# Putting the gate block of the first group ahead of its row tiles, in the opening of a hybrid decoder kernel

## The chip, the cores and the metric

The kernel runs on one core of a Trainium2 chip. The metric is the device time of one execution in microseconds. All weights and activations are float32 in memory. The engines named below are TensorE (PE, its weight loads PEld), VectorE (DVE), ScalarE (ACT), GpSimd (POOL) and SyncE (SP), which issues the weight loads.

## What is computed

The reference is a two-layer decoder trunk on 256 tokens of width 2048: a Mamba-2 layer, an MLP, an attention layer with a sliding window, an MLP, each followed by a layer norm. Only the start matters here, the Mamba-2 mixer:

```python
zxbcdt = h @ w_in                     # (256 x 2048) @ (2048 x 10304)
z   = zxbcdt[..., :D_INNER]           # the gate
xbc = zxbcdt[..., D_INNER:D_INNER + CONV_DIM]
dt_raw = zxbcdt[..., D_INNER + CONV_DIM:]
xbc = jax.nn.silu(conv(xbc) + conv_b) # causal, 4 taps, per channel
dt  = jax.nn.softplus(dt_raw + dt_bias)
...                                   # scan in two chunks of 128 tokens
y = y * jax.nn.silu(z)
```

The channels fall into 8 groups. Each has 128 channels of B, 128 of C, 512 of xs and 512 of z. The 64 values of dt are needed by all groups.

## The kernel before

**Products in split float32.** Each operand is split into a high part, which is the value rounded to the type fp32r, and a low part, the rest. A product is high times high, high times low and low times high. The weights pass in chunks of 128 x 1024 values (512 KB): SP loads chunk k into one of four slots of `raw` (L346 to L354), ACT copies it to `whi` (L818), DVE subtracts to get `wlo` (L1249), PE uses it. `whi` and `wlo` are rings of eight chunks. The semaphore `w_split` counts chunks that DVE has finished. SP waits for it before it loads into a slot again, so the load of chunk k is issued once chunk k - 4 is split; PE waits for it in `chunk()` (L426). ACT splits chunk k (`step`, L820) once PE has used chunk k - 8 (`w_used`).

**Two kinds of product.** `row_tile` (L431) makes 128 output channels for all 256 tokens in one PSUM bank, from two chunks: 16 matmuls of 512 columns (L451) and 16 of 256 columns (L457). Its weight chunk holds 8 blocks of 128 rows x 128 columns, so its load moves in pieces of 512 B. `column_block` (L481) makes 512 channels, tokens on partitions, in two banks, from eight chunks of 256 rows x 512 columns; `column_chunk_products` (L461) issues twelve matmuls of 512 columns for each (L476 to L478). Row tiles give B, C, xs and dt, column blocks give z.

**The opening.** PE first multiplies zeros (L552), then turns x: the input lies in SBUF as tokens x channels, and PE transposes it in tiles of 128 x 128 (L528) into PSUM, from where ACT writes its high part and DVE its low part to `actA` (`x_hi` L838, `x_lo` L1272). `x_transposes(g)` (L532) turns one quarter of x, 512 channels of both token halves, eight transposes into two banks. Quarters 0 and 1 are turned before the first product, 2 and 3 inside the first row tile. SP issues x quarter 0, the identity, chunk 0, quarters 1 and 2, chunk 1, quarter 3 (L366 to L379), then waits for quarter 2 before chunk 2. POOL waits for quarter 2 before it issues its nine small loads of vectors (L1970 on).

**The first group** (PE L620, ACT L940, DVE L1457): row tiles for B, C and dt, four for xs, then the z block. The first row tiles add their low products chunk by chunk (`lo_last=False`). Inside the second tile PE transposes the small vectors (L538). Between the chunks of the z block it transposes dt (`dt_transposes`, after chunk 0), makes its sums over time (`dt_sums`, after chunk 4), and transposes those (`cs_transposes`, after chunk 6).

What follows a row tile is a chain: ACT copies the half of the bank with the cross products (`cross`, L888), DVE adds the other half, which frees the bank (`conv_sum`, L1368), DVE runs the four taps (`conv`, L1375), ACT takes the tanh, DVE makes the silu (`silu`, L1392). xs tiles alternate between banks 0 and 1. For dt: `dt_cross` and `dt_add` (L1315), PE transposes, `softplus` on DVE (L1322 to L1354, some 18 small operations one after the other), PE's `dt_sums`, DVE's copy (L1356), PE's `cs_transposes`, then POOL writes the sums to memory and reads them back spread over all partitions (L1950). For z: ACT takes the tanh (`z_tanh`, L905), DVE multiplies (`z_out`, L1397).

Each engine's order is written out by hand, as a list of `step()` (one chunk's split) and these pieces. An engine that waits in one piece holds up all that is listed behind it.

**The later groups** (`group`, PE L631, ACT L985, DVE L1503): six row tiles, then the z block. After its first row tile a group takes the `s1` products of the group before (L586), which need all six `silu` of that group. After its fourth it takes the scan products (L595), which need ACT's `decay` (L915), which needs the sums read back by POOL. The z of the group before is taken through tanh at the head of the next group.

Of the kernel before, what the change touches and what calls it, by code (L numbers as in the profile page):

```python
# [29 lines left out]
P = 128  # L30
T = 256
# [95 lines left out]
def build(nc, t, out):  # L127
# [57 lines left out]
    per_head_in = nc.alloc_semaphore("per_head_in")  # L185
    x_in = [nc.alloc_semaphore(f"x_in{g}") for g in range(4)]
# [7 lines left out]
    by_dma = {keys_doubled, rows_out, rows_in, *loaded, *x_in, ident_in, consts_in, vectors_in, per_head_in, x_again_in, gains_in, out_done}  # L194
# [118 lines left out]
    def group_chunks(g, first=False):  # L313
        cols = [COL_B + g * DS, COL_C + g * DS] + [COL_XS + g * GW + i * P for i in range(4)]
        if first:
            cols.insert(2, COL_DT - NHD)
        for c in cols:
            for r in range(2):
                yield t["w_in"], r * CH, c, P
        for r in range(8):  # L320
            yield t["w_in"], r * 2 * P, COL_Z + g * GW, BLK
# [16 lines left out]
    with block:  # L338
# [3 lines left out]
        def _(e):  # L342
# [18 lines left out]
            def load_x(g):  # L361
                cols = slice(g * BLK, (g + 1) * BLK)
                e.dma_start(xin[:, :, cols], t["x"][0, :, cols].rearrange("(h p) n -> p h n", p=P)).then_inc(
                    x_in[g], C.up(x_in[g]))

            def load_first_group():  # L366

                load_x(0)
                e.dma_start(ident[:, :], t["consts"][:, K_ID:K_ID + P]).then_inc(ident_in, C.up(ident_in))
                for k, args in enumerate(group_chunks(0, first=True)):  # L370
                    load(*args)
                    if k == 0:
                        load_x(1)
                        load_x(2)
                    if k == 1:
                        load_x(3)
                        e.wait_ge(x_in[2], C.now(x_in[2]))
# [37 lines left out]
        def _(e):  # L415
# [15 lines left out]
            def row_tile(b, act, ready={}, inside={}, first=False, lo_last=True):  # L431
# [5 lines left out]
                for h in range(2):  # L437
                    if first and h == 0:
                        s = 0
                        e.wait_ge(first_split, C.next(first_split))  # L440
                    else:
                        s = chunk()
                    for k in range(8):
                        kt = 8 * h + k
                        if first and kt == 4:
                            s = chunk()
# [14 lines left out]
            def column_chunk_products(b0, act, c, ready=0, inside={}, second_half=None):  # L461
# [3 lines left out]
                s = chunk()  # L465
                order = [(k, h) for h in range(NH) for k in range(2)] if second_half else [
                    (k, h) for k in range(2) for h in range(NH)]
                for i, (k, h) in enumerate(order):
                    if i in inside:
                        inside[i]()  # L470
                    if i == 2 and second_half:
                        second_half()
                    kt = 2 * c + k
# [58 lines left out]
            def x_transposes(g):  # L532
                e.wait_ge(x_in[g], C.next(x_in[g]))
                for h in range(NH):
                    transposes(2 + (2 * g + h) % 6,
                               [xin[:, h, (4 * g + i) * P:(4 * g + i + 1) * P] for i in range(4)], counted=False)
# [21 lines left out]
            zero_products(8)  # L558
# [249 lines left out]
        def _(e):  # L808
# [29 lines left out]
            def x_hi(g):  # L838
                for h in range(NH):
                    b = 2 + (2 * g + h) % 6  # L840
# [1227 lines left out]
```

## Time and profile before

| | before |
|---|---|
| median of 3 runs | 2385.74 us (2385.48 to 2387.28) |
| the profiled execution | 2385.26 us |
| its span in the trace | 2383.1 us |
| PE busy | 2366.2 us, 99% |
| VectorE busy | 1576.4 us, 66% |
| ScalarE busy | 1168.7 us, 49% |
| weight loads | 818 of 512 KB |
| DMA traffic | 455 MB, mean 191 GB/s |

The profiled execution has 2.2 us outside its span. PE's busy share is near the whole, so time can only be won or lost where PE stands still or where it does something other than the products. All times in the rows are counted from the start of the span.

### The profile page before, as it was taken

What the parts mean: (1) busy time and instruction counts of PE and PEld (TensorE: products, weight loads), DVE (VectorE), ACT (ScalarE), POOL (GpSimd) and SP (SyncE); (2) the same over time, 40 slices, a digit from 0 to 9 for tenths busy, and PEclk for the clock granted to TensorE, in tenths of its full rate; (3) what the DMA queues carried; (4) which work ended last, traced back from release to release, by engine and by line L of the source; (5) the groups of instructions that cost most, each with busy time, mean ns of one, the idle gap of its engine ahead of it and who ended that gap; (6) DMA issues with size and microseconds to landing.
All of it is one profiled execution on the core that took longest, in us unless ns stands there. A gap on an engine that the chain in (4) does not pass through costs nothing.

```text
span 2383.1 us, 32530 instructions
## 1 busy us (share of the span) xinstructions
PE 2366.2 (99%) x12610; PEld 1999.4 (84%) x12610; DVE 1576.4 (66%) x2151; ACT 1168.7 (49%) x1742; POOL 40.8 (2%) x85
## 2 busy tenths in 40 slices
PE   9999999999999999999999999999999999999998
PEld 8888888888888888888888888778888888888886
DVE  7888888885568556556556577766864654655655
ACT  5555555564355444445344355774543443443441
POOL 0000000000000000000000000000000000000000
PEclk9999999999999999999999999999999999999999
DMA  8766666657667666666666646446776666666663
GB/s 235 228 195 194 187 192 189 190 171 238 194 187 234 210 189 189 197 187 188 198 189 188 200 153 203 125 124 202 199 232 188 190 196 184 192 198 188 191 195 109
DMA packets 487826, 455.08 MB, mean 191 GB/s; under 512 B 13792, under 2 KB 360080, under 8 KB 485392
## 3 DMA queue, kind: packets, MB, share of 16 engines
q1 hardware_dynamic: 484608, 433.51, 61.2%
q0 software_dynamic: 3088, 19.79, 2.4%
q8 instruction: 88, 1.44, 0.3%
q14 instruction: 42, 0.34, 0.0%
HBM read 450.55 MB, written 2.16 MB: 190 GB/s over the span
## 4 chain that ended last, share of the span: by engine, by line
PE 92%; DVE 3%; ACT 2%; DMA 1%; issue 1%; SPq 0%; POOL 0%; DVEq 0%; ACTq 0%
PE ps L451 25%; PE ps L476 15%; PE ps L477 15%; PE ps L478 15%; PE ps L457 13%; PE ps L509 2%; PE ps L507 2%; PE ps L508 2%; DVE wlo L1249 1%; PE ps L528 1%; ACT whi L818 1%; PE ps L600 1%; ACT pb L1172 0%; DMA csb<-cs_rows 0%; ACT em L920 0%
## 5 line engine op out<-in xcount | busy, mean ns | idle before, releaser
L1249 DVE TENSOR_TENSOR wlo<-raw,whi 128x1024 fp32r<-128x1024 f32 x817 | 994.4, 1222 | 670.2 <-ACT whi L818 669.0
L818 ACT ACTIVATE whi<-raw 128x1024 fp32r<-128x1024 f32 x817 | 859.6, 1057 | 852.5 <-PE ps L478 447.9
L451 PE MATMUL ps<-actA,whi 128*128 128x512 f32 x2704 | 648.2, 391 | 0.8 <-DVE wlo L1249 0.5
L451 PEld LDWEIGHTS ps<-actA,whi 128*128 128x128 f32 x2704 | 497.1, 188 | 98.6 <-issue 0.9
L476 PE MATMUL ps<-whi,actB 128*128 128x512 f32 x1056 | 412.7, 391 | 0.0
L477 PE MATMUL ps<-wlo,actB 128*128 128x512 f32 x1056 | 411.0, 389 | 0.0
L478 PE MATMUL ps<-whi,actB 128*128 128x512 f32 x1056 | 410.9, 389 | 0.0
L457 PEld LDWEIGHTS ps<-actA,wlo 128*128 128x128 f32 x2704 | 347.2, 191 | 13.5
L457 PE MATMUL ps<-actA,wlo 128*128 128x256 f32 x2704 | 351.3, 283 | 0.0
L476 PEld LDWEIGHTS ps<-whi,actB 128*128 128x128 f32 x1056 | 198.3, 188 | 42.7 <-issue 1.3
L478 PEld LDWEIGHTS ps<-whi,actB 128*128 128x128 f32 x1056 | 198.3, 188 | 41.3
L477 PEld LDWEIGHTS ps<-wlo,actB 128*128 128x128 f32 x1056 | 198.3, 188 | 40.3
L476 PE MATMUL ps<-whi,actA 128*128 128x512 f32 x544 | 215.9, 397 | 1.0 <-DVE actA L1261 1.0
L478 PE MATMUL ps<-whi,actA 128*128 128x512 f32 x544 | 212.0, 390 | 0.0
L477 PE MATMUL ps<-wlo,actA 128*128 128x512 f32 x544 | 212.0, 390 | 0.0
L476 PEld LDWEIGHTS ps<-whi,actA 128*128 128x128 f32 x544 | 102.1, 188 | 23.6 <-issue 2.5
L478 PEld LDWEIGHTS ps<-whi,actA 128*128 128x128 f32 x544 | 102.1, 188 | 21.8
L477 PEld LDWEIGHTS ps<-wlo,actA 128*128 128x128 f32 x544 | 102.3, 188 | 19.6
L832 ACT ACTIVATE actB<-fsq 128x256 fp32r<-128x256 f32 x120 | 50.2, 418 | 109.9 <-DVE fsq L1727 109.9
L1578 DVE TENSOR_TENSOR res<-ps,res 128x512 f32<-128x512 f32 x80 | 51.9, 686 | 63.0 <-PE ps L509 32.6
L903 ACT ACTIVATE thb<-xh 128x256 f32<-128x256 f32 x48 | 19.9, 415 | 123.8 <-DVE xh L1389 123.8
L1727 DVE SCALAR_TENSOR_TENSOR fsq<-fb 128x256 f32<-128x256 f32 x120 | 51.0, 425 | 4.1
(209 smaller groups left out, 1679.5 us busy)
## 6 DMA issues: line engine op xcount, KB each, us to landing
raw<-in_mlp_w SPq DMA_DIRECT2D x512, 512.0 KB, 4.5
raw<-in_a_w_in SPq DMA_DIRECT2D x162, 512.0 KB, 4.6
raw<-in_a_w_out SPq DMA_DIRECT2D x64, 512.0 KB, 4.7
raw<-in_b_w_q SPq DMA_DIRECT2D x32, 512.0 KB, 5.1
raw<-in_b_w_o SPq DMA_DIRECT2D x32, 512.0 KB, 4.1
csb<-cs_rows POOLq DMA_DIRECT2D x8, 1024.0 KB, 6.9
raw<-in_kv_w SPq DMA_DIRECT2D x16, 512.0 KB, 4.0
gb<-in_ln_g POOLq DMA_DIRECT2D x4, 1024.0 KB, 7.8
```

Of the source, the lines that this page charges most:

```text
L451: e.matmul(ps[:, b, :], whi[:, s, k * P:(k + 1) * P], act[:, kt, :, :].rearrange("p a n -> p (a n)"), start=(kt == 0), stop=False)
L457: last = e.matmul(ps[:, b, T:2 * T], wlo[:, slots[half], k * P:(k + 1) * P], act[:, kt, 0, :], start=False, stop=(kt == KT - 1))
L476: e.matmul(ps[:, b0 + h, :], act[:, kt, 0, tk], whi[:, s, w], start=(kt == 0), stop=False)
L477: e.matmul(ps[:, b0 + h, :], act[:, kt, 0, tk], wlo[:, s, w], start=False, stop=False)
L478: last = e.matmul(ps[:, b0 + h, :], act[:, kt, 1, tk], whi[:, s, w], start=False, stop=(kt == KT - 1))
L507: e.matmul(ps[:, b0 + h, :], act[:, kt, 0, tk], hi_w, start=(kt == 0), stop=False)
L508: e.matmul(ps[:, b0 + h, :], act[:, kt, 0, tk], lo_w, start=False, stop=False)
L818: e.activation(whi[:, s, :], raw[:, r, :], ACT.Copy).then_inc(w_hi_done, C.up(w_hi_done))
L832: e.activation(dst, src, ACT.Copy).then_inc(act_hi_done, C.up(act_hi_done))
L1249: e.tensor_tensor(wlo[:, s, :], raw[:, r, :], whi[:, s, :].bitcast(F32), ALU.subtract).then_inc(w_split, C.up(w_split))
L1578: ins = e.tensor_tensor(r, ps[:, b, :], r, ALU.add)
L1727: e.scalar_tensor_tensor(fsq[:, i % 2, :], fb[:, i % 2, :], 0.0, fb[:, i % 2, :], ALU.max, ALU.mult).then_inc(f_squared, C.up(f_squared))
```

## The change

In the first group the z block comes first, then the row tiles in the order dt, B, C, xs 0 to 3. x is turned in eight pieces of 256 channels (four transposes into one bank), the first two before the first product and each later one in front of the chunk before its use. The first x piece and the first half of chunk 0 are loaded separately. dt's transposes follow B, its sums follow xs 0, their transposes follow xs 1. All row tiles now add their low products last. In the second group the z pieces fall away, since z of the first is taken inside the first group.

```diff
 def group_chunks(g, first=False):
     cols = [COL_B + g * DS, COL_C + g * DS] + [COL_XS + g * GW + i * P for i in range(4)]
...
+    z = [(t["w_in"], r * 2 * P, COL_Z + g * GW, BLK) for r in range(8)]
+    rows = [(t["w_in"], r * CH, c, P) for c in ([COL_DT - NHD] if first else []) + cols for r in range(2)]
+    yield from z + rows if first else rows + z
...
 SP, load_first_group
-    load_x(0)
-    e.dma_start(ident[:, :], ...)
-    for k, args in enumerate(group_chunks(0, first=True)):
-        load(*args)
-        if k == 0:
-            load_x(1)
-            load_x(2)
-        if k == 1:
-            load_x(3)
-            e.wait_ge(x_in[2], C.now(x_in[2]))
+    chunks = list(group_chunks(0, first=True))
+    load_x(slice(0, 2 * P), x_first_in)
+    load_first_half(0, first_loaded)
+    e.dma_start(ident[:, :], ...)
+    load_first_half(1, loaded[0])
+    load_x(slice(2 * P, 4 * P), x_in[0])
+    for k in range(1, 4):
+        load(*chunks[k])
+        load_x_quarter(k)
+    for k in range(4, len(chunks)):
+        load(*chunks[k])
...
 PE
+def x_transposes(m):
+    ...
+    transposes(4 + m % 4, [xin[:, h, (2 * m + i) * P:(2 * m + i + 1) * P] for i in range(2) for h in range(NH)],
+               counted=False)
 x_transposes(0)
-zero_products(8)
+zero_products(4)
 x_transposes(1)
+def first_z_block():
+    fill(2)
+    fill(3)
+    for c in range(8):
+        if 0 < c < 7:
+            x_transposes(c + 1)
+        column_chunk_products(2, actA, c, 1, first=(c == 0))
 def first_group():
-    row_tile(0, actA, ready={0: 2, 4: 2, 8: 2, 12: 2}, first=True, lo_last=False,
-             inside={2: lambda: x_transposes(2), 7: lambda: x_transposes(3)})
-    row_tile(1, actA, inside={8: vector_transposes}, lo_last=False)
-    row_tile(4, actA, lo_last=False)
-    for i in range(4):
-        row_tile(i % 2, actA, lo_last=i > 0)
-    column_block(2, actA, after={0: [dt_transposes], 4: [dt_sums], 6: [cs_transposes]})
+    first_z_block()
+    row_tile(4, actA, inside={8: vector_transposes})
+    row_tile(0, actA)
+    dt_transposes()
+    row_tile(1, actA)
+    row_tile(0, actA)
+    dt_sums()
+    row_tile(1, actA)
+    cs_transposes()
+    row_tile(0, actA)
+    row_tile(1, actA)
...
 ACT and DVE, opening
+for m in range(1, 6):
+    x_hi(m)            # DVE: x_lo(m)
+    split_weights()
+for m in (6, 7):
+    x_hi(m)            # DVE: x_lo(m)
+    step()
...
 ACT, first_group, as it stands after the change
+for _ in range(6):
+    step()
+z_tanh(8)
+step(); step()
+dt_cross(10); step(); constants_out(); step()
+cross(0, 12); step(); tanh(0); dt_exp(); step()
+cross(1, 14); step(); tanh(1); step()
+cross(2, 16); step(); tanh(2); dt_decays(); step()
+cross(3, 18); step(); tanh(3); dt_cs2(); step()
+cross(4, 20); step(); tanh(4); step()
+cross(5, 22); tanh(5)
...
 DVE, first_group, as it stands after the change
+for _ in range(6):
+    step()
+z_out()
+step(); step()
+vectors_out()
+...                    # cwg copy
+dt_add()
+step(); step()
+conv(0, 0); step()
+softplus(); step()
+silu(0, 0); conv(1, 0); step(); step()
+silu(1, 0); conv(2, 0); dt_sums(); step(); step()
+silu(2, 0); conv(3, 0); rotations_out(); step(); step()
+silu(3, 0); conv(4, 0); step(); step()
+silu(4, 0); conv(5, 0); silu(5, 0)
```

(The two lists of ACT and DVE are written several calls to a line here; in the file each stands on its own line.)

## Rows read from the trace of the kernel before

**Rows 1.** The page: span, and busy time with share of the span.
```profile
span 2383.1 us, 32530 instructions
PE 2366.2 (99%) x12610; PEld 1999.4 (84%) x12610; DVE 1576.4 (66%) x2151; ACT 1168.7 (49%) x1742; POOL 40.8 (2%) x85
```

**Rows 2.** Timeline, 1 to 10 us: start, duration, engine, line, operation, count, idle before.
```profile
1.07 4.52 PE L552 MATMUL ps<-st 128*128 128x128 f32 x24 [1.07 <-DVE st L1279]
...
5.43 1.04 PE L528 MATMUL ps<-ident,xin 128*128 128x128 f32 x8
6.07 1.09 ACT L832 ACTIVATE actA<-ps 128x512 fp32r<-128x512 f32 x2 [4.03 <-PE ps L528]
...
6.77 1.29 DVE L1261 TENSOR_TENSOR actA<-ps,actA 128x512 fp32r<-128x512 f32 x2 [5.74 <-ACT actA L832]
7.04 0.63 ACT L846 ACTIVATE whi<-raw 128x512 fp32r<-128x512 f32 x1
...
7.98 1.28 DVE L1284 TENSOR_TENSOR wlo<-raw,whi 128x512 fp32r<-128x512 f32 x2
...
8.49 1.09 PE L528 MATMUL ps<-ident,xin 128*128 128x128 f32 x8 [0.24 <-DMA xin<-in_x]
...
9.34 0.71 PE L451 MATMUL ps<-actA,whi 128*128 128x512 f32 x2
```

**Rows 3.** Timeline of PE: the vectors' transposes, a row tile, block and groups beginning.
```profile
20.94 0.48 PE L542 MATMUL ps<-ident,vst 48*128 48x48 f32 x5
...
21.79 2.12 PE L451 MATMUL ps<-actA,whi 128*128 128x512 f32 x8
...
42.34 3.82 PE L451 MATMUL ps<-actA,whi 128*128 128x512 f32 x16
...
53.48 0.40 PE L476 MATMUL ps<-whi,actA 128*128 128x512 f32 x1
...
76.50 3.79 PE L451 MATMUL ps<-actA,whi 128*128 128x512 f32 x16
...
137.96 3.79 PE L451 MATMUL ps<-actA,whi 128*128 128x512 f32 x16
...
198.64 1.52 PE L451 MATMUL ps<-actA,whi 128*128 128x512 f32 x6
```

**Rows 4.** Timeline of ACT, second group: the wait for the sums read back.
```profile
91.80 2.45 ACT L920 ACTIVATE em<-csb,csg 128x128 f32<-128x128 f32 x8 [1.00 <-DMA csb<-cs_rows]
```

**Rows 5.** Windows, 6 to 8 us: length, busy of each engine, PEclk, DMA share, GB/s.
```profile
6.00:8.00 2.00, 2.00 (x21) 2.00 (x19) 1.23 (x3) 1.93 (x4) 0.00 (x0) 1.00 1.02 356
```

**Rows 6.** Timeline of SP and ACT, 67 to 80 us: a load and three waits of ACT.
```profile
67.72 0.37 SPq L351 DMA_DIRECT2D raw<-in_a_w_in  x1
...
71.78 1.06 ACT L818 ACTIVATE whi<-raw 128x1024 fp32r<-128x1024 f32 x1 [2.22 <-DMA raw<-in_a_w_in]
74.41 1.06 ACT L818 ACTIVATE whi<-raw 128x1024 fp32r<-128x1024 f32 x1 [1.56 <-DMA raw<-in_a_w_in]
...
79.41 1.06 ACT L818 ACTIVATE whi<-raw 128x1024 fp32r<-128x1024 f32 x1 [0.53 <-DMA raw<-in_a_w_in]
```

**Rows 7.** Timeline of DVE: pieces of its list.
```profile
22.14 0.21 DVE L1299 TENSOR_SCALAR cw<-ps 128x32 f32<-128x32 f32 x1
...
24.18 0.42 DVE L1382 TENSOR_SCALAR xh<-xpad,cwg 128x256 f32<-128x256 f32 x1
...
60.24 0.28 DVE L1325 TENSOR_TENSOR dv<-ps,dtb 128x128 f32<-128x128 f32 x1
...
66.47 2.36 DVE L1249 TENSOR_TENSOR wlo<-raw,whi 128x1024 fp32r<-128x1024 f32 x2
...
84.36 1.28 DVE L1401 SCALAR_TENSOR_TENSOR zs<-yb,ps 128x512 f32<-128x512 f32 x2
...
108.56 0.42 DVE L1372 TENSOR_TENSOR xpad<-ps,xpad 128x256 f32<-128x256 f32 x1
...
111.24 1.22 DVE L1249 TENSOR_TENSOR wlo<-raw,whi 128x1024 fp32r<-128x1024 f32 x1
```

More of the change, by code:

```diff
@@ L437, in row_tile @@
                 for h in range(2):
[L438 to L442, printed above, removed]
+                    s = chunk()
                     for k in range(8):
                         kt = 8 * h + k
-                        if first and kt == 4:
-                            s = chunk()
                         if kt and kt in ready:
@@ L472, in column_chunk_products @@
                         second_half()
+                    if first and i == 2:
+                        s = chunk()
                     kt = 2 * c + k
@@ L529, in transposes @@
                 last.then_inc(full[b], C.up(full[b]))
[L532 to L536, printed above, removed]
+            def x_transposes(m):
+                if m == 0:
+                    e.wait_ge(x_first_in, C.next(x_first_in))
+                elif m == 1:
+                    e.wait_ge(x_in[0], C.next(x_in[0]))
+                elif m % 2 == 0:
+                    e.wait_ge(x_in[m // 2], C.next(x_in[m // 2]))
+                transposes(4 + m % 4, [xin[:, h, (2 * m + i) * P:(2 * m + i + 1) * P] for i in range(2) for h in range(NH)],
+                           counted=False)
             def vector_transposes():
@@ L903, in tanh, with z_tanh @@
                 e.activation(thb[:, i % 2, :], xh[:, i % 2, :], ACT.Tanh).then_inc(tanh_done, C.up(tanh_done))
-            def z_tanh():
-                products()
+            def z_tanh(used=None):
+                if used is None:
+                    products()
+                else:
+                    e.wait_ge(w_used, used)
                 for c in range(NH):
@@ L968, in first_group, with group @@
                 step()
-                cross(5, 14)
+                cross(5, 22)
+                tanh(5)
+            def group(par, z=True):
                 step()
-                tanh(5)
-                step()
-                step()
-                dt_exp()
-                for _ in range(4):
-                    step()
-                C.n[full[4]] += 1
-                dt_decays()
-                step()
-                step()
-                step()
-                dt_cs2()
-                step()
-            def group(par):
-                step()
-                z_tanh()
+                if z:
+                    z_tanh()
                 step()
@@ L1024, in _ @@
             before = dict(C.n)
-            group(0)
+            before[z_tanh_done] -= NH
+            group(0, z=False)
             with C.loop(3, before, 2):
@@ L1270, in per_head, with x_lo @@
                 return x[:, bass.ds(g * GH, GH)].unsqueeze(2).broadcast_to([P, GH, HD])
[L1272 to L1277 removed]
+            def x_lo(m):
+                b = 4 + m % 4
+                e.wait_ge(full[b], C.next(full[b]))
+                lo(actA[:, 2 * m:2 * m + 2, 1, :], ps[:, b, :].rearrange("p (t n) -> p t n", n=T),
+                   actA[:, 2 * m:2 * m + 2, 0, :])
             e.memset(st[:, 0:P], 0.0).then_inc(zeros_ready, C.up(zeros_ready))
@@ L1288, in _ @@
             split_first_chunk()
-            x_lo(1)
-            x_lo(2)
-            split_weights()
-            x_lo(3)
+            for m in range(1, 6):
+                x_lo(m)
+                split_weights()
+            for m in (6, 7):
+                x_lo(m)
+                step()
             def vectors_out():
@@ L1490, in first_group, with group @@
                 conv(5, 0)
-                step()
                 silu(5, 0)
-                step()
-                step()
-                softplus()
-                step()
-                step()
-                dt_sums()
-                rotations_out()
-                for _ in range(6):
-                    step()
-            def group(g, par):
+            def group(g, par, z=True):
                 step()
@@ L1508, in group @@
                 step()
-                z_out()
+                if z:
+                    z_out()
                 step()
@@ L1548, in _ @@
             before = dict(C.n)
-            group(1, 1)
+            for sem, n in ((z_tanh_done, NH), (free[2], 1), (free[3], 1)):
+                before[sem] -= n
+            group(1, 1, z=False)
             with C.loop(3, before, 2) as i:
```

106 lines of the change are left out of this document (52 added, 54 removed).

## The prediction

> **What bounds the kernel now.** I read the page first: PE is busy for 99% of the span [rows 1]. So the sum of the products sets the time, and a change of order can only win or lose where PE waits. The change touches the first two groups, up to 199 us. There I read the timeline engine by engine.
>
> What the reader is to see, in order. The first product starts at 9.34, and the turning ahead of it waited for x until 8.49 [rows 2]. Two whole row tiles take 53.48 - 42.34 = 11.14, so 5.57 each; one 512-column matmul starts every (3.82 - 0.39)/15 = 0.23 [rows 3]. The first group ends at 76.50, the second lasts 61.46 and the third 60.68 [rows 3]. The difference of 0.8 lies at the scan products, which came late because the sums were read back late: ACT waited 1.00 for them [rows 4]. From 9.34 to 76.50 are 67.2 us; seven tiles (39.0), eight chunks of z at 2.72 (21.8), 16 transposes of x (half of 8.49 to 9.34 per four, 0.43, so 1.7), the vectors' transposes (0.85, 20.94 to 21.79 [rows 3]) and the dt pieces (23.0 of the block less 21.8, so 1.2) make 64.6. PE thus waits some 2.6 us there, and 0.8 in the second group. No change of order can win more than this and the earlier start.
>
> **The start.** Four transposes are enough for the first product now, from one bank. They start at 5.4 as before, since twelve zero products last until 5.59 [rows 2]. ACT's copy of one bank takes half of 1.09, so the half chunk is split on ACT at 6.6, not 7.04, and on DVE at 7.5, not 7.98; with 0.65 for it PE starts at 8.2 [rows 2]. The second x piece must be there by then: 1.1 MB lie up to it in the queue, where 1.6 MB lay ahead of 8.49 [rows 2]; the difference is 1.5 us at 356 GB/s [rows 5], so it lands near 7.0. **Gain 1.1.** The four zero products less lie in a wait and cost nothing. x's later pieces and the 2 KB pieces of z's chunks ask for 786 KB per 3.2 us, 246 GB/s, below the 356 measured; I cost them at nothing, and up to 0.8 once if GpSimd's small loads, now issued some 3 us later and into the same stretch, slow them.
>
> **The z block.** 24 transposes instead of 16 follow the first product: six times 0.46, 2.8. Chunk m is split only after ACT has copied x piece m: 0.64 from PE's first transpose to ACT, 0.55, then 1.06 on ACT and 1.2 on DVE [rows 2, 6, 7], 3.6 with the hops. PE covers it with two turnings and a chunk, 0.46 + 2.72 + 0.46 = 3.6. At the last chunk one turning is missing, so it waits 0.4. End: 8.2 + 21.8 + 2.8 + 0.4 = 33.2.
>
> **The row tiles, PE alone.** dt with the vectors' transposes until 39.7, B until 45.2, then dt's transposes, C, xs 0, sums, xs 1, transposes, xs 2, xs 3. With nothing to wait for PE would be done at 33.2 + 39.0 + 0.9 + 1.1 = 74.2, 2.3 ahead of 76.50.
>
> **VectorE's list** is what I expect to end last. The softplus, 6.23 us on DVE (60.24 to 66.47 [rows 7]), stood in the z block, where PE needs 2.72 per chunk and DVE only 1.2. Now it stands between row tiles, where two splits (2.3) and a convolution with its silu (108.56 to 111.24, 2.68 [rows 7]) already take 5.0 of 5.57. Nor does DVE come in with a lead: z_out stands behind the split of chunk 13. The splits of chunks 6 and 7 hang on the last x pieces, at 27.3 and 30.6. The load of 11 is issued at 30.6. A load lands 4.1 after its issue (67.72 to 71.78), the following ones on average 1.9 apart (71.78 to 79.41, four steps [rows 6]), I take 2.0: 34.7, 36.7 and chunk 13 at 38.7. ACT 1.1, DVE 1.2: z_out begins at 41.0.
>
> From there the list runs back to back: z_out 1.2; chunks 14 and 15, 2.3 and a wait of 0.5 for 15; vectors 2.0 (22.14 to 24.18 [rows 7]); dt's sum 0.5, done at **47.5**. Chunks 16, 17, 2.3; convolution 2.3; chunk 18, 1.2; softplus 6.2, done at **59.5**. Chunk 19 and silu 1.5, then the sum that frees bank 1, 0.4, at **61.4**. The rest of that convolution 1.9, chunks 20, 21 and 0.4 for ACT, silu and convolution 2.7, the copy of dt's sums 0.3, done at **69.1**.
>
> PE against this: it is at dt's transposes at 45.2 and waits until 47.6, **2.4**. It comes to the sums at 59.0, waits **0.6**, and after them waits for bank 1 from 60.2 until 61.4, **1.2**. xs 1 ends at 67.0 and the last transposes wait for the copied sums until 69.2, **2.2**. Then 0.2 and two tiles: 80.6, which is 4.1 behind 76.50.
>
> **The second group.** Its first tile ends at 86.2; the sixth silu comes at 86.9 by the same list (six splits, three silu-convolution pairs, tanh and the turn to ACT), a wait of **0.7**. The 0.8 at the scan products goes, since the sums are out 8 us before this group begins, not 1 us after. z_tanh and z_out are only moved. After that each engine finds the same list as before.
>
> **The sum.** 4.1 + 0.7 - 0.8 = +4.0. Against the profiled execution, 2385.26, that is 2389.3; the median of the runs lies 0.48 above it, so 2389.7. Bounds: loads only as far apart as 356 GB/s makes them (1.5 [rows 5]) bring z_out to 40.0 and the sum to +3.0; loads 2.63 apart (71.78 to 74.41 [rows 6]) delay the chunks up to 17 and with them the list by 2.7, so +6.7. By the Trainium skill (DMA: Bandwidth & Descriptors, Anatomy of one DMA) a transfer costs about 2.0 us and its bytes at 436 GB/s, 3.2 us for 512 KB and 1.2 apart; the trace has 4.1 and 1.9. By its figures z_out would begin near 38.3 and the sum would be about +1.3, an estimate; the trace decides.
>
> **Rivals.**
> *The list keeps up.* If DVE's pieces cost less here than alone, or loads run ahead, all four waits go: 74.2 instead of 76.50 and 0.8 more, -3.1, 2382.6. For it: DVE has 28.1 us of work from z_out to the copied sums, PE 29.6 from the block's end to where it needs them. Against it: PE is 7.8 us into that when z_out starts, and each piece is priced from a row.
> *TensorE's clock falls, slower.* The order leaves PE standing 2.4 and 2.2 us. The granted clock reads 1.00, the 2.4 GHz level [rows 5], yet the first 24 pieces of the zero products last 4.52 [rows 2], where at the pace of turning x (eight in 1.04) they would take 2.9; so 1.6 us were lost at the first start. Should both pauses cost this again, the sum is +7.2, 2392.9. It decides once a pause is long enough; no row of the opening shows a wait of PE over 1.1 once it has begun, so the trace cannot say. The Trainium skill (TensorE: Matmul & The Clock Gate, Why this matters for your kernels) says that longer gaps in PE's work bring the clock down to its lower level; no run here shows that yet.
> *Loads fall behind, slower.* With the loads 2.63 apart and 0.8 lost in the z block: +7.5, 2393.2.
> *The start is not early.* If the second x piece comes as late as before, the first product stays at 9.3 and all shifts: +5.1, 2390.8.
>
> **The numbers.** A measurement here tells 0.2% from no change, 4.8 us. The forecast (DVE's list is late, +2.2 to +6.7) gets 0.65; the list that keeps up 0.12; the clock 0.08; the loads 0.10; the late start 0.05. Slower by over 4.8: a quarter of the forecast's 0.65 (0.16) and the three slow rivals (0.22): 0.38. Faster by over 4.8 would need more than all that PE waits for, 0.02. The rest, 0.60, lies within 0.2%. The range from 2386.6 (+0.9) to 2393.4 (+7.7) leaves out the first rival and a little above.
>
> **What the new profile would show.** Right: first product near 8.2; PE at dt's transposes waiting on DVE for about 2 us; waits before the sums, before xs 1 and before the last transposes; the second group's first tile near 80.6; VectorE without a gap from 41 to 80. Wrong: z_out beginning before 38, or PE without a wait between 34 and 75; then my price of the loads or of the list is off. If the second group starts near 80 but the total does not move by 4, something later gave it back.

## The result, and the profile after

The changed kernel takes 2390.67 us in the median of 20 runs (2389.20 to 2391.75). The kernel before, beside it on the same chip, takes 2386.71 us (2384.98 to 2389.79, 20 runs). The ratio is 1.0016, with a 95% interval of 1.0010 to 1.0022. That is slower by 2.4 to 5.3 us, and 3.96 us between the medians. The ratio of 0.16% lies within the 0.2% that the prediction had set as its bound; its interval reaches 0.22%. The profiled execution took 2390.39 us, against 2385.26 before.

The page of the changed kernel, span and busy times, to be laid beside [rows 1]:

```profile
span 2388.3 us, 32524 instructions
PE 2367.9 (99%) x12602; PEld 1999.6 (84%) x12602; DVE 1576.6 (66%) x2151; ACT 1167.8 (49%) x1742; POOL 41.1 (2%) x85
```

The span grew by 5.2. DVE and ACT did the same work. PE is busy for 1.7 more, although it has eight instructions fewer. So 3.5 of the growth is waiting, and 1.7 is busy time in which no more work was done. Both show in the timeline of PE in the changed kernel (start, duration, engine, line, operation, count, idle before and what ended it). Here are the opening, then the first group's row tiles, then the starts of the second and third group:

```profile
7.81 0.66 PE L535 MATMUL ps<-ident,xin 128*128 128x128 f32 x4 [0.84 <-DMA xin<-in_x]
8.25 0.47 PE L483 MATMUL ps<-whi,actA 128*128 128x512 f32 x1
...
12.24 0.47 PE L483 MATMUL ps<-whi,actA 128*128 128x512 f32 x1 [0.51 <-DVE wlo L1272]
...
34.26 1.98 PE L452 MATMUL ps<-actA,whi 128*128 128x512 f32 x8
...
48.27 0.44 PE L535 MATMUL ps<-ident,dth 128*128 128x128 f32 x2 [1.64 <-DVE small L1343]
48.47 3.92 PE L452 MATMUL ps<-actA,whi 128*128 128x512 f32 x16
...
60.26 0.66 PE L582 MATMUL ps<-dv,kst 128*128 128x64 f32 x4 [0.39 <-DVE dv L1376]
...
62.06 5.53 PE L452 MATMUL ps<-actA,whi 128*128 128x512 f32 x16 [0.92 <-DVE xpad L1396]
...
69.74 0.41 PE L593 MATMUL ps<-ident,cs 128*64 128x128 f32 x2 [0.24 <-DVE small L1385]
...
81.14 3.82 PE L452 MATMUL ps<-actA,whi 128*128 128x512 f32 x16
...
87.13 1.09 PE L535 MATMUL ps<-ident,xT 128*128 128x128 f32 x8 [0.26 <-DVE xT L1418]
...
108.80 3.92 PE L452 MATMUL ps<-actA,whi 128*128 128x512 f32 x16 [0.32 <-DVE xpad L1396]
...
142.72 3.79 PE L452 MATMUL ps<-actA,whi 128*128 128x512 f32 x16
```

The first product is at 8.25, where [rows 2] had 9.34, and the second z chunk, at 12.24, waited 0.51 for its split. The z block ends and dt's tile begins at 34.26. Then come the four waits that the prediction had named, all ended by VectorE: 1.64, 0.39, 0.92 and 0.24. The second group begins at 81.14 (76.50 in [rows 3]). The third begins at 142.72 instead of 137.96. The delay is 4.64 at the second group and 4.76 at the third and, by the same timeline, at the fourth (203.40 instead of 198.64). So it was made in the first group, and the second gave nothing back.

One line has an odd duration. The 16 matmuls at 62.06 last 5.53, and the 16 at 48.47 last 3.92. The windows of the changed kernel around it (window, length, busy time of each engine, granted clock of TensorE, DMA share, GB/s):

```profile
58.00:60.00 2.00, 1.87 (x16) 1.66 (x14) 1.77 (x7) 0.00 (x0) 0.00 (x0) 1.00 0.00 0
60.00:62.00 2.00, 0.88 (x6) 0.74 (x6) 2.00 (x4) 0.00 (x0) 0.00 (x0) 1.00 0.00 0
62.00:64.00 2.00, 1.94 (x6) 1.49 (x7) 1.86 (x6) 0.00 (x0) 0.00 (x0) 0.64 0.68 166
64.00:66.00 2.00, 2.00 (x6) 1.61 (x5) 1.71 (x3) 1.94 (x4) 0.00 (x0) 0.51 0.34 101
66.00:68.00 2.00, 2.00 (x12) 1.70 (x12) 1.93 (x5) 0.64 (x1) 0.00 (x0) 1.00 0.79 207
```

The granted clock fell to 0.5, the 1.2 GHz level, after PE had been busy for only 0.88 of the two microseconds ahead of it. It came back before 66. This cost 5.53 - 3.92 = 1.6, nearly all of the 1.7 by which PE's busy time grew. The rival of the falling clock thus happened. Yet the second group begins only 0.5 behind the forecast, and an experiment had to show why.

The other two engines of the changed kernel. ACT waits for loads while PE is in the first two row tiles:

```profile
35.54 1.06 ACT L841 ACTIVATE whi<-raw 128x1024 fp32r<-128x1024 f32 x1 [1.86 <-DMA raw<-in_a_w_in]
38.18 1.06 ACT L841 ACTIVATE whi<-raw 128x1024 fp32r<-128x1024 f32 x1 [1.58 <-DMA raw<-in_a_w_in]
39.93 1.06 ACT L841 ACTIVATE whi<-raw 128x1024 fp32r<-128x1024 f32 x1 [0.69 <-DMA raw<-in_a_w_in]
```

VectorE comes behind it. From 42 to the copied sums at 69.3 its timeline has no gap over 0.38, which is a wait for ScalarE inside the softplus. Here are z_out, dt's sum, the softplus, the sum that frees bank 1, and the copied sums:

```profile
42.16 1.28 DVE L1425 SCALAR_TENSOR_TENSOR zs<-yb,ps 128x512 f32<-128x512 f32 x2
...
47.67 0.42 DVE L1341 TENSOR_TENSOR dth<-ps,dth 128x256 f32<-128x256 f32 x1
...
53.89 0.28 DVE L1349 TENSOR_TENSOR dv<-ps,dtb 128x128 f32<-128x128 f32 x1
...
60.13 1.22 DVE L1272 TENSOR_TENSOR wlo<-raw,whi 128x1024 fp32r<-128x1024 f32 x1
...
61.60 0.41 DVE L1396 TENSOR_TENSOR xpad<-ps,xpad 128x256 f32<-128x256 f32 x1
...
69.28 0.28 DVE L1382 COPY cs<-ps 128x128 f32<-128x128 f32 x1
```

In the next 394 us nothing differs: PE is busy for 392.85 in the changed kernel (206 to 600) and 393.03 before (201.4 to 595.4). The two profiled executions are 5.1 apart, so some 0.4 more lies further on; it was not traced.

### The profile page after: what moved, and what is told of

The parts are those of the page before. It is cut to its first block, busy times and chain, and to the rows that moved or that the text cites. A ratio compares the mean times of both kernels' runs of the same rounds, so it can differ in the third digit from the quotient of the medians.

```text
span 2388.3 us, 32524 instructions
## 1 busy us (share of the span) xinstructions
PE 2367.9 (99%) x12602; PEld 1999.6 (84%) x12602; DVE 1576.6 (66%) x2151; ACT 1167.8 (49%) x1742; POOL 41.1 (2%) x85
## 3 DMA queue, kind: packets, MB, share of 16 engines
HBM read 450.55 MB, written 2.16 MB: 190 GB/s over the span
## 4 chain that ended last, share of the span: by engine, by line
PE 91%; DVE 4%; ACT 2%; DMA 1%; issue 1%; SPq 0%; POOL 0%; DVEq 0%; ACTq 0%
PE ps L452 24%; PE ps L483 15%; PE ps L484 15%; PE ps L485 15%; PE ps L458 12%; PE ps L516 2%; PE ps L514 2%; PE ps L515 2%; DVE wlo L1272 2%; PE ps L535 1%; DMA raw<-in_a_w_in 1%; ACT whi L841 1%; PE ps L611 1%; DVE xh L1410 0%; ACT pb L1195 0%
```

## The experiments

Two things were open. Is it VectorE's list that puts the second group at 81, or each wait by itself, or the loads? And what did the fall of the clock cost? Twelve kernels ran, the two of the comparison once more among them. All ratios are to the kernel before on the same chip.

**1. The order inside the list.** dt's sum goes ahead of the vectors' pieces on VectorE:

```diff
 DVE, first_group
+dt_add()
 vectors_out()
 ...                    # cwg copy
-dt_add()
```

> The changed kernel with one piece moved in VectorE's list: dt's sum stands ahead of the vectors' copies, not behind them, so that PE's wait before dt's transposes (1.6 us in the changed kernel) goes. If VectorE's list sets the end, nothing is won: the list is as long as before up to the copied sums, PE waits longer at the later places, the second group still starts within 0.4 us of 81.1 and the time is that of the changed kernel. If PE's waits simply add up, each a loss of its own, the second group starts at 79.5 and the time is 1.6 us less.

Measured: ratio 1.0013 (1.0004 to 1.0023), median 2390.34. The timeline of PE, first group:

```profile
46.69 0.38 PE L535 MATMUL ps<-ident,dth 128*128 128x128 f32 x2
...
60.15 0.66 PE L582 MATMUL ps<-dv,kst 128*128 128x64 f32 x4 [1.94 <-DVE dv L1376]
...
61.95 5.53 PE L452 MATMUL ps<-actA,whi 128*128 128x512 f32 x16 [0.92 <-DVE xpad L1396]
...
69.64 0.41 PE L593 MATMUL ps<-ident,cs 128*64 128x128 f32 x2 [0.24 <-DVE small L1385]
```

The wait of 1.64 before dt's transposes is gone, and the one before the sums grew from 0.39 to 1.94, by 1.55. The marks behind it are where they were within 0.12, up to the second group at 81.02 (81.14). PE reached the next thing sooner and waited there for the same end of the softplus. The four waits are one debt, seen at four places.

**2. Work for PE in the middle waits.** Products of zeros into a free bank, three before the sums and four behind them:

```diff
 PE, first_group
 row_tile(0, actA)
+spare_products(3)
 dt_sums()
+spare_products(4)
 row_tile(1, actA)
```

> The changed kernel with seven products of zeros more on PE, three ahead of dt's sums over time and four behind them, in the stretch where PE waits and after which its granted clock falls to 0.50 for some 3.5 us (first half of the tile xs 1, which lasts 1.7 us longer). Expected: the clock stays at 1.00 in that tile, it lasts 5.6 us and not 7.4. If VectorE's list sets the end, the wait ahead of the last transposes grows from 0.2 to about 2 us, the second group starts within 0.4 us of 81.1 and the fall of the clock has cost nothing. If the fallen clock costs time, the second group starts 1.7 us earlier.

Measured: 1.0014 (1.0005 to 1.0024), median 2390.59. The tile xs 1 ran at full clock (16 matmuls in 3.92). Then, in PE's timeline:

```profile
69.25 0.41 PE L598 MATMUL ps<-ident,cs 128*64 128x128 f32 x2 [1.85 <-DVE small L1392]
69.41 5.52 PE L452 MATMUL ps<-actA,whi 128*128 128x512 f32 x16
...
82.25 3.82 PE L452 MATMUL ps<-actA,whi 128*128 128x512 f32 x16
```

PE came 2.1 sooner to the last transposes (1.6 by the clock, 0.5 since xs 1 began sooner in this profile) and waited for the copied sums: 1.85, where the prediction had 2.2 and the changed kernel 0.24. So in the changed kernel the slow stretch had run while PE would have waited anyway. Here the fall came behind the last wait, where nothing covers it, and the second group began at 82.25, 1.1 later. The third began at 142.95, only 0.2 later. The second group has slack: it lasts 61.58 in the changed kernel and 60.70 here, so 0.9 of a late start is taken back in it.

**3. A shorter list.** Five of the six steps of the softplus' polynomial are left out (the outputs that depend on dt are other values):

```diff
-for k in (13, 11, 9, 7, 5, 3):
+for k in (3,):
```

> The changed kernel with five of the six steps of the softplus polynomial left out (the output differs in its logarithm's series), 1.63 us less in VectorE's list. If the list sets the end, all marks behind it move by that much: copied sums near 68.0 and not 69.6, the second group at 79.5, the time 1.6 us less. If the loads or PE's own work set the end, the second group stays within 0.4 us of 81.1.

Measured: 1.0009 (1.0000 to 1.0019), median 2389.47. In this profile dt's tile began at 34.58, and VectorE's list was 0.85 behind that of the changed kernel when the softplus began (54.74 against 53.89). The copied sums came at 68.50 instead of 69.28. With the late start taken out, the list is shorter by 0.78 + 0.85 = 1.63, the whole of what was removed. So the list comes off its end as the theory has it. The forecast of the second group at 79.5 was missed all the same: PE waited 1.83 before the last transposes, then the clock fell (16 matmuls in 5.51), and the second group began at 81.95, the third at 142.64 (142.72 in the changed kernel). The gain of the median, 1.2 against the changed kernel, is within what the intervals leave open. That a shorter list makes the whole time shorter is thus not shown.

**4 and 5. z_out back in the second group, alone and with the first edit.**

```diff
 DVE, first_group
 for _ in range(6):
     step()
-z_out()
 step()
 step()
...
-group(1, 1, z=False)
+group(1, 1)
```

> The changed kernel with one piece of VectorE's list moved: the product with z's tanh (two operations, 1.28 us in the timeline of the changed kernel) leaves the place behind the split of chunk 13 and goes back to the head of the second group. Theory: VectorE's list is what ends last in the first group, so everything behind this piece comes 1.1 to 1.2 us earlier, the copied sums at 68.1 instead of 69.3. TensorE waits about 0.4 before dt's transposes instead of 1.64, and at most 0.4 in all before the sums and xs 1; with no fall of its clock it would be at the last transposes at 66 to 67 and wait there 1.3 to 2. The second group begins at 79.9 to 80.1 instead of 81.1. If the clock falls behind that last wait, 1.7 us are lost again, and the second group begins at 81 to 81.8; the median then moves by less than 1 us. The rival, that the loads and not the list set the first group, expects the copied sums where they are (69.3), since chunks 14 and 15 are then waited for instead: no change in any mark beyond 0.3 us. Median by the theory 2388.9 to 2390.5, by the rival 2390.7.

> Both moves together in the changed kernel: the product with z's tanh goes to the second group, and dt's sum stands ahead of the vectors' pieces. Theory of the list: TensorE does not wait at all before dt's transposes; the first wait is at the dt sums or at bank 1, 0.7 to 1.7 us, and the last transposes come at about 68.2; second group near 80.0, or 1.7 later where the clock falls behind the last wait. Both moves together give no more than the first alone at the end of the list (softplus ends at the same time in both), so the median equals that of the other kernel of this pair within 0.5 us. If waits were added up one by one, this kernel would be 1.6 us faster than the other.

Measured: 1.0022 (1.0013 to 1.0032) with median 2391.76, and 1.0022 (1.0013 to 1.0031) with median 2390.96. The theory failed here, and its rival was right. With 1.28 of work taken out ahead of them, the vectors' pieces began at 46.09 (45.63 in the changed kernel), and the copied sums came at 69.76, not 68.1. The loads of this profile came some 0.6 later (38.79 against 38.18 for chunk 12), so against them the list gained 0.1 and not 1.2. ACT and DVE of the kernel with z_out moved, ahead of the vectors' pieces:

```profile
38.79 1.06 ACT L841 ACTIVATE whi<-raw 128x1024 fp32r<-128x1024 f32 x1 [2.28 <-DMA raw<-in_a_w_in]
40.59 1.06 ACT L841 ACTIVATE whi<-raw 128x1024 fp32r<-128x1024 f32 x1 [0.74 <-DMA raw<-in_a_w_in]
...
43.86 1.06 ACT L841 ACTIVATE whi<-raw 128x1024 fp32r<-128x1024 f32 x1 [0.29 <-DMA raw<-in_a_w_in]
```

```profile
39.88 1.23 DVE L1272 TENSOR_TENSOR wlo<-raw,whi 128x1024 fp32r<-128x1024 f32 x1 [2.11 <-ACT whi L841]
41.68 1.23 DVE L1272 TENSOR_TENSOR wlo<-raw,whi 128x1024 fp32r<-128x1024 f32 x1 [0.58 <-ACT whi L841]
43.60 2.58 DVE L1272 TENSOR_TENSOR wlo<-raw,whi 128x1024 fp32r<-128x1024 f32 x2 [0.69 <-ACT whi L841]
```

VectorE waits 0.69 for the next chunk in the place where z_out stood, and 0.23 more inside the following pair (2.58 for two splits; two back to back last 2.35). So the loads set this part: with four slots each load waits for an earlier split, and z_out had filled a gap. The changed kernel's own trace agrees: ScalarE ended its split of chunk 15 at 44.35 (43.29 and 1.06), and VectorE began its own near 44.5 (the second of the pair at 43.36 above), so without z_out it could not have begun more than 0.15 sooner. Only behind chunk 15, at 45.6, is it the list that sets the end. In the kernel with both moves PE did not wait before dt's transposes, and waited 2.46 before the sums: the debt moved on, as in the first experiment. The two kernels have the same ratio; their medians are 0.8 apart, more than the 0.5 that I had allowed and half of the 1.6 that waits adding up one by one would make. The traces decide it rather than the times: the second group begins at 81.63 and 81.85.

**6 and 7. Work for PE in all four waits.** As in 2, with products also before dt's transposes and before the last ones, all into bank 3: first 10 and 12 of them, then 6 and 6.

```diff
+spare_products(10)     # 6
 dt_transposes()
...
+spare_products(12)     # 6
 cs_transposes()
```

> The changed kernel with products of zeros in all four of TensorE's waits of the first group: 10 before dt's transposes, 3 before the dt sums, 4 behind them, 12 before the last transposes. They take about 0.13 us each (eight in 1.06 in the timeline of the changed kernel), less than the waits they stand in (1.64; 0.39; 0.92; 1.85 in the kernel with spare products at the middle two places alone). Nothing else changes. Theory: the clock's fall, 1.7 us, comes when TensorE stands still here, and VectorE's list sets the end: with the fall avoided everywhere the copied sums still come at 69.3, the last transposes follow at once, and the second group begins at 80.4 to 80.8 (81.14 in the changed kernel, 82.25 in the kernel that filled the middle two alone). The median is 2390 to 2391, since 0.5 us cannot be told. Rival: the falls come at random and not from the waits; then a fall is seen in some tile though no wait is left above 0.4, and the second group begins above 82.

> As the kernel with products of zeros in all waits, but 6 before dt's transposes and 6 before the last ones, since one product took 0.236 us there (12 in 2.84, two instructions each), twice what I had assumed, and 12 of them ended 0.95 behind the copied sums. Theory: no fall of the clock, no product that ends behind what it covers, and from the start of dt's tile to the start of the second group 46.5 to 46.9 us, against 47.68 with too many, 46.88 in the changed kernel (where the fall lay under VectorE's list), 49.05 in its second profile (where one fall lay behind the last wait). Rival: a fall happens all the same, then 48 or more. Median 2389.8 to 2390.8, and less spread than the changed kernel's 2389.7 to 2393.3.

Measured: 1.0019 (1.0010 to 1.0028) for both, medians 2391.38 and 2390.83. No fall of the clock is seen in either. My price of a spare product was wrong in the first: one is two instructions, so 12 last 2.84 and ended 0.95 behind the copied sums. Its second group began at 82.67 and not at 80.8 or sooner. PE in the kernel with the sized ones:

```profile
46.73 1.50 PE L568 MATMUL ps<-st 128*128 128x128 f32 x12
48.52 0.44 PE L535 MATMUL ps<-ident,dth 128*128 128x128 f32 x2 [0.29 <-DVE small L1352]
...
62.31 3.94 PE L452 MATMUL ps<-actA,whi 128*128 128x512 f32 x16
...
68.00 1.50 PE L568 MATMUL ps<-st 128*128 128x128 f32 x12
70.00 0.41 PE L598 MATMUL ps<-ident,cs 128*64 128x128 f32 x2 [0.50 <-DVE small L1394]
...
81.39 3.82 PE L452 MATMUL ps<-actA,whi 128*128 128x512 f32 x16
```

Its second group begins at 81.39, 46.87 behind dt's tile (34.52). In the changed kernel that distance is 81.14 - 34.26 = 46.88. So the fall in its profile cost nothing: with it or without it, PE goes on when VectorE has copied the sums. In time the products of zeros gained nothing: the median is that of the changed kernel, and the spread (2389.87 to 2392.70) hardly less than in its repetition (2389.72 to 2393.28), where I had expected less.

**8 and 9. Both kernels once more, unedited.**

> The changed kernel once more, unedited, to see how much its marks move between executions. Second x piece waited for 0 to 1.7 us and the first product between 8.2 and 9.3, as in the seven profiles of this study that begin in the same way; if the first profile (8.25) was typical the gain of the start is 1.1, if it was the luckiest, about 0.6. Clock: one fall of about 1.7 us somewhere between 48 and 75 us. Fourth group between 203.2 and 204.3. Median 2390 to 2391.

> The kernel before once more, unedited: first product at 9.3 if its start is fixed by the load of x, anywhere from 9.0 to 10 if it varies as that of the changed kernel does. No fall of the clock after 10 us. Second group at 76.4 to 77.2, third at 137.9 to 138.7. Median 2386 to 2387.

Measured: 1.0014 (1.0005 to 1.0023) with median 2391.18, and 0.9998 (0.9989 to 1.0007) with median 2386.39. Both profiles differ from the first ones more than I had expected. The changed kernel, PE:

```profile
9.24 0.47 PE L483 MATMUL ps<-whi,actA 128*128 128x512 f32 x1 [0.32 <-DVE wlo L1306]
...
49.49 0.44 PE L535 MATMUL ps<-ident,dth 128*128 128x128 f32 x2 [2.16 <-DVE small L1343]
49.68 5.52 PE L452 MATMUL ps<-actA,whi 128*128 128x512 f32 x16
...
70.96 0.41 PE L593 MATMUL ps<-ident,cs 128*64 128x128 f32 x2 [1.81 <-DVE small L1385]
71.13 5.52 PE L452 MATMUL ps<-actA,whi 128*128 128x512 f32 x16
```

The first product is at 9.24, and the clock fell twice. The first fall was covered by the list. The second was not, and the second group began at 84.00, the fourth at 205.39 (203.40 in the first profile). This execution took 2393.28, 2.9 more than the first one profiled. The kernel before, PE:

```profile
1.07 5.49 PE L552 MATMUL ps<-st 128*128 128x128 f32 x24 [1.07 <-DVE st L1279]
...
9.97 0.72 PE L451 MATMUL ps<-actA,whi 128*128 128x512 f32 x2
...
29.08 2.11 PE L451 MATMUL ps<-actA,whi 128*128 128x512 f32 x8 [1.16 <-DVE wlo L1249]
32.65 2.06 PE L451 MATMUL ps<-actA,whi 128*128 128x512 f32 x8 [0.52 <-DVE wlo L1249]
```

Its first 24 zero products last 5.49 instead of 4.52. The first product is at 9.97, later tiles wait 1.16 and 0.52 for a split, the second group begins at 78.05 (76.50 before) and the third at 139.98 (137.96). So an opening alone moves by 1 to 2 us from one execution to the next, in both kernels, and a single pair of profiles cannot price the start. The distance between the kernels held: at the third group 4.76 in the first pair, 144.71 - 139.98 = 4.73 in this one.

**10 to 12. A middle way.** Five chunks of z come first, so the early product stays. The row tiles follow, with the last three z chunks between them, and z's tanh and product go back to the second group. The lists of ACT and DVE and the order of the loads follow. The softplus again has z chunks beside it.

```diff
 PE, first_group
-first_z_block()
-row_tile(4, actA, inside={8: vector_transposes})
-row_tile(0, actA)
-dt_transposes()
-row_tile(1, actA)
-row_tile(0, actA)
-dt_sums()
-row_tile(1, actA)
-cs_transposes()
-row_tile(0, actA)
-row_tile(1, actA)
+for c in range(5):
+    ...
+    column_chunk_products(2, actA, c, 1, first=(c == 0))
+row_tile(0, actA, ready={0: 3})
+row_tile(1, actA, inside={8: vector_transposes})
+row_tile(4, actA)
+row_tile(0, actA)
+row_tile(1, actA)
+dt_transposes()
+row_tile(0, actA)
+column_chunk_products(2, actA, 5)
+dt_sums()
+column_chunk_products(2, actA, 6)
+row_tile(1, actA)
+cs_transposes()
+column_chunk_products(2, actA, 7)
...
 DVE, end of first_group, in the second form (third form: both steps ahead of conv(5, 0); ACT: a step between tanh(4) and tanh(5) in both)
 silu(3, 0)
+step()
 conv(5, 0)
 step()
 silu(4, 0)
 silu(5, 0)
-step()
```

> Another order of the first group: only five chunks of the z block come first (with x in eight pieces and the early start of the change), then the tiles B, C, dt, xs 0 to 2 with the other three chunks of z between them, so that the softplus stands beside chunks that ask little of VectorE; the z pieces of ScalarE and VectorE stay in the second group as in the kernel before. If the loss of the change lies in VectorE's list alone and its early start and fuller use of the first loads are a gain, PE waits for under 1 us after the first product, the second group starts between 73.5 and 75 (76.5 before, 81.1 with the change) and the time is 2 to 3 us under the kernel before. If early z itself costs (its loads, its transposes), the second group starts at 76.5 or later.

> The order with five z chunks first, and VectorE's last pieces before the second group reordered: the split ahead of the sixth silu goes ahead of the sixth convolution (ACT's tanh gets behind its split to match). In the run of the first form the load of the third chunk of the second group was issued at 80.16 and ScalarE waited 4.60 us for it, since VectorE had done one split only between 74.4 and 78.9. Theory: what gave the 1.2 us back in the second group is this gap in the issue of loads; now a load is issued near 76 instead of 78.4 and the next near 79.4, the wait of 4.60 shrinks below 3.5, TensorE's waits in the second group fall from 1.5 to under 1, the third group begins at 137.2 to 137.7 instead of 137.99, and the median is 0.3 to 0.8 below the first form's ratio of 0.9997, that is 0.9994 to 0.9996. Rival: the memory's rate sets it (the sums are read back, 1 MB, in the same stretch); then the load lands as late as before and the third group begins at 138.0.

> As the kernel before this, with two splits ahead of the sixth convolution instead of one. By the theory of the gap the loads are issued near 74.5, 76 and 77.2, so they come still earlier, but the sixth silu ends near 80.7, about where TensorE needs it (80.9 in the first form): a wait of 0 to 0.5 there. Third group at 137.0 to 137.7. By the rival, the memory's rate, 138.0 as before; and if the sixth silu is late by more than 1 us the second group loses that and the third begins at 138.5.

Measured, in the same order: 0.9997 (0.9988 to 1.0006), 0.9994 (0.9985 to 1.0003) and 0.9995 (0.9986 to 1.0004), medians 2386.06, 2385.30 and 2384.82. In the first form the waits before the dt pieces are gone, and the second group began at 75.29, 1.2 ahead of [rows 3], if not at 75 or sooner as forecast. So the waits go when the softplus has z chunks beside it again. But the third began at 137.99, where the first profile of the kernel before is at 137.96: against that one, all of it was given back. The lines of PE in that second group, first form:

```profile
94.23 3.92 PE L452 MATMUL ps<-actA,whi 128*128 128x512 f32 x16 [0.59 <-DVE xpad L1404]
...
102.60 1.15 PE L611 MATMUL ps<-xdt,em 128*64 128x64 f32 x32 [0.60 <-DVE em L1457]
104.07 3.92 PE L452 MATMUL ps<-actA,whi 128*128 128x512 f32 x16 [0.32 <-DVE xpad L1404]
```

I had put this down to a gap in the issue of loads. The second form closed the gap (a load issued at 76.09 instead of 78.36), ACT's wait fell from 4.60 to 3.21, and the first of these waits from 0.59 to 0.36. The third group still began at 137.95, since PE waited 0.59 for `em` as before. The second group lasted 62.50, against 62.70 in the first form and 61.46 in [rows 3], so the gap in the loads explains 0.2 of a loss of 1.24, and the forecast was missed. In the third form the opening was late (first product 9.09, second group 76.59, third 138.45), so its profile does not decide; its second group lasted 61.86. What bounds the second group there, beside VectorE's work (54.4 of 62.5 us busy in the second form), stays open. Against the second profile of the kernel before, with its third group at 139.98, all three forms are 1.5 to 2.0 ahead, so the profiles do not settle whether they gain. No version is shown to beat the kernel before, since all three intervals reach 1.

## Why the prediction was right, and where its steps were not

**The sum.** Forecast 2389.7 with a range of 2386.6 to 2393.4; measured 2390.67, and 2391.18 in the repetition. The forecast difference was +4.0 and the medians are 3.96 apart; the absolute time is 1.0 higher because the kernel before has 2386.71 in 20 runs and had 2385.74 in the three that the forecast started from. The likeliest case held: VectorE's list is late, PE stands at the dt pieces, and the delay is made in the first group. The first experiment showed that the waits are one debt, the third that 1.63 off the list behind 54 comes off its end in full, the tenth that the waits go when the softplus stands beside z chunks. That the number fits so closely is partly luck: the marks of both pairs of profiles are 4.7 to 4.8 apart at the third group, and several terms missed in both directions, as follows.

**The start.** Forecast 8.2, measured 8.25, a gain of 1.09 in this pair. The nine profiles with this same opening (the changed kernel twice and the seven kernels of experiments 1 to 7) have it at 8.25, 8.29, 8.42, 8.61, 8.87, 8.87, 8.97, 9.03 and 9.24, the three of experiments 10 to 12 at 8.68, 9.09 and 9.33, and two of the kernel before at 9.34 and 9.97. So the first product does come earlier, but 8.25 is the earliest of twelve, and that the size was met to 0.05 is luck.

**The z block.** Forecast end 33.2, measured 34.26; mis-sized by 1.06. A chunk with its turning was priced well: chunks begin at 15.42, 18.65, 21.87, 25.05 and 28.27, 3.2 apart, where I had 2.72 + 0.46. The miss is the second chunk. PE turned the next piece of x from 11.08 on and, at 0.4 for that, could have begun the chunk at 11.5. It began at 12.24, since the split was late: ScalarE had waited 0.68 for this chunk's load, until 9.77. I had left the early loads at nothing, and that term was too low by some 0.8. At the last chunk PE waited 0.22, where I had 0.4. This also says what the early start is worth. In the nine profiles the second chunk begins between 12.05 and 12.92, in no order with the first product (12.24 behind 8.25, 12.05 behind 8.87), and the block ends 22.0 to 22.1 behind it. Of the 1.1 won at the first product, 0.8 was handed back at the second chunk.

**VectorE's list.** Its marks came 0.5 to 1.2 late, and from dt's sum on the spacing was right:

| mark | forecast | measured | in the repetition |
|---|---|---|---|
| z_out begins | 41.0 | 42.16 | 43.37 |
| dt's sum done | 47.5 | 48.1 | 49.3 |
| sum that frees bank 1 done | 61.4 | 62.0 | 63.2 |
| copied sums done | 69.1 | 69.6 | 70.8 |

The first is the price of the loads. ACT began the splits of chunks 11, 12 and 13 at 35.54, 38.18 and 39.93: 2.64 and 1.75 apart, and I had taken 2.0 twice. By the figures of the Trainium skill (DMA: Bandwidth & Descriptors, Anatomy of one DMA) z_out would have begun near 38.5, an estimate (30.6 + 3.2 + 2 x 1.2 + 2.3; the prediction's 38.3 is a slip), which was further off. That section gives them for transfers that GpSimd issues, and these loads are issued by SyncE. The trace of the changed kernel again shows 4.2 from the issue of the first of these loads (31.33) to ACT. One step was wrong in kind. I charged z_out's 1.2 to the list, but experiments 4 and 5 show that it lay in a gap that the loads leave. That it stands there costs next to nothing.

**PE's waits.** Forecast 2.4, 0.6, 1.2 and 2.2; measured 1.64, 0.39, 0.92 and 0.24. The first three are smaller because PE itself was late, by 1.4 at dt's transposes (46.6 against 45.2), while the list was only about 0.6 late. The last is smaller by 2.0, of which 1.6 is xs 1 at the fallen clock. Second group: forecast 80.6, measured 81.14.

**The second group.** I had expected 0.7 lost at `s1` and 0.8 won at the scan products. Measured: 0.26 of wait before the transposes for `s1`, with 0.4 lost there in all, and 0.36 won at the scan products (106.35 to 108.80, where the kernel before has 101.21 to 104.02). PE's wait of 0.19 for `em` is gone, but the one of 0.32 behind it, for VectorE's sum, stayed. So the prediction was wrong to put the whole 0.8 down to the sums read back late; less than half of it was that. The two misses cancel: the group lasts 61.58, against 61.46 in [rows 3].

**The rivals.** *The list keeps up* fell, with waits in every profile of the changed order. *TensorE's clock falls* was given 0.08, and in the trace it happened: after the waits of this order the granted clock went from 1.00 to 0.5 for some 3.4 us, 1.6 us lost each time (2.4 in the kernel with both moves). The Trainium skill (TensorE: Matmul & The Clock Gate, Why this matters for your kernels) says that long gaps in PE's work bring the clock down to its lower level. The lower level is what the trace shows, but here it came behind shorter gaps than that section warns of, and not behind each of them, so the measurement decides. The price was right, but my rival added it to the sum, which is true only of a fall behind the last wait. That the profiled fall had a wait behind it is luck; whether the executions without a profile had falls, and where, is not known. *Loads fall behind* was half right: loads were slower than forecast once, by 0.6. *The start is not early* did not happen in the first profile, and nearly did in the repetition. (The three slow rivals add up to 0.23, not 0.22.)

## What to carry to other kernels

Where one engine runs through a fixed list, the waits of the others on it are not separate costs. Price the list from end to end, look at the last wait, and expect that removing an earlier one only moves it. An engine that stands still, or runs slowly, ahead of a wait that comes anyway costs nothing; the same behind the last wait delays what follows by its full length, until slack further on takes part of it back (0.9 of 1.6 here). An early start is worth only what the next thing to arrive lets through: look at the second chunk, not at the first product. Two profiles are two executions: before a gain of 1 us at the start is believed, look at the opening in several.

## What the runs showed of the hardware

Whether the granted clock falls is not decided by the length of a single wait alone. These are the waits of PE for VectorE in the first group, by profile:

| kernel | waits and what followed |
|---|---|
| changed | 1.64: none; 0.39 and 0.92: fall |
| changed, repetition | 2.16: fall; 1.81: fall |
| dt's sum first | 1.94 and 0.92: fall; 0.24: none |
| spare products in the middle | 1.21: none; 1.85: fall |
| short softplus | 2.17: none; 1.83: fall |
| z_out late | 2.07: fall; 1.86: none |
| both moves | 2.46: fall, already in the small products ahead of the wait of 0.37 (16 matmuls in 6.34) |
| spare products in all waits, too many | no waits, none |
| spare products in all waits, sized | 0.29 and 0.50: none |

Of the seven waits of 1.81 to 2.17 with nothing beside them, five were followed by a fall and two were not, so it cannot be counted on either way. With products of zeros in all the waits no fall was seen in two profiles, and the time did not change. The kernel before, with waits up to 1.16, shows none in two profiles. After a fall the 16 matmuls of 512 columns last 5.5 instead of 3.9; with both moves 6.34, and the clock reads 0.50 to 0.68 from 60 to 68 there, so the slow stretch was longer.

The first 24 zero products of the program last 4.5 us in one execution and 5.5 in another of the same kernel ([rows 2] and experiment 9), and 4.35 to 5.49 in the fourteen profiles. The opening is not a fixed time.
